# The causal mask of the attention: added by VectorE in the instruction that finds the maximum, instead of by matmuls on TensorE

## The reference

```
for i in range(S // Q_BLOCK):                 # 8 blocks of 128 queries
    q0 = i * Q_BLOCK
    end = q0 + Q_BLOCK                        # keys up to the block's own end
    s = einsum('bqhcd,bkhcd->bhcqk', q[:, q0:end], k[:, :end]) * scale
    causal = kpos[None, :] <= qpos[:, None]
    p = softmax(where(causal, s, -inf), axis=-1)
    w = p[:, :, 0] - lam * p[:, :, 1]
    outs.append(einsum('bhqk,bkhe->bqhe', w, v[:, :end]))
```

## Time and profile before

| | |
|---|---|
| runs | 3737.33, 3740.36, 3741.08 us; median 3740.36 |
| span of the profiled execution, first to last instruction | 3738.0 us |
| the profiled execution's own time | not listed apart from its span; the runs above lie from 0.7 below to 3.1 above that span |
| TensorE busy | 3485.4 us, 93% of the span, 16158 matmuls |
| weight loads | 2816.6 us, beside the matmuls |
| VectorE, ScalarE, GpSimd busy | 1433.6, 829.6 and 949.5 us |
| mean granted TensorE clock | 0.953 of full speed |
| chain of waits, by engine | TensorE 81%, VectorE 12%, ScalarE 2%, issue 2%, DMA 1% |

### The profile page before, as it was taken

How to read it: one execution, slowest core, us unless ns; L and a number is a source line. 1 busy time by engine, 2 the same in 40 slices (tenths; PEclk the granted TensorE clock), 3 DMA queues, 4 the chain that set the end, 5 groups by cost and what they waited for, 6 DMA issues and landing times.

```text
span 3738.0 us, 42270 instructions
## 1 busy us (share of the span) xinstructions
PE 3485.4 (93%) x16158; PEld 2816.6 (75%) x16158; DVE 1433.6 (38%) x1753; ACT 829.6 (22%) x1308; POOL 949.5 (25%) x514
## 2 busy tenths in 40 slices
PE   6888999999889798899999999979999989999999
PEld 5666777777668386677888888868878768888887
DVE  6774444444520557642012222321621543223231
ACT  3332232333320232232122222221110011101010
POOL 2222111111023131112322212224323323333332
PEclk9898999999889799989999999989999989999999
DMA  3432000000001211111121212232111211111112
GB/s 137 126 115 87 23 29 23 23 29 23 12 28 50 107 45 51 51 57 40 50 91 54 66 48 71 52 113 63 50 39 50 86 33 51 45 50 46 49 50 73
DMA packets 83681, 213.93 MB, mean 57 GB/s; under 512 B 7024, under 2 KB 33264, under 8 KB 83456
## 3 DMA queue, kind: packets, MB, share of 16 engines
q1 hardware_dynamic: 48176, 167.27, 14.2%
q10 hardware_dynamic: 35408, 45.24, 3.9%
HBM read 193.44 MB, written 19.04 MB: 57 GB/s over the span
## 4 chain that ended last, share of the span: by engine, by line
PE 81%; DVE 12%; ACT 2%; issue 2%; DMA 1%; PEld 0%; ACTq 0%; DVEq 0%; PEldq 0%; POOL 0%; SPq 0%; POOLq 0%
PE proj_bank L207 20%; PE proj_bank L209 19%; PE proj_bank L208 19%; PE aux_banks L719 3%; PE aux_banks L207 2%; PE aux_banks L209 2%; PE aux_banks L208 2%; PE aux_banks L785 1%; PE aux_banks L729 1%; PE aux_banks L1702 1%; PE aux_banks L514 1%; DVE lru_conv L602 1%; PE aux_banks L1385 1%; PE aux_banks L722 1%; DVE ada_acc L591 1%
## 5 line engine op out<-in xcount | busy, mean ns | idle before, releaser
L207 PE MATMUL proj_bank<-h_hi,slab_hi 128*128 128x512 f32 x2816 | 1131.5, 402 | 36.3 <-DVE h_lo L372 9.1
L208 PE MATMUL proj_bank<-h_lo,slab_hi 128*128 128x512 f32 x2816 | 1111.0, 395 | 0.0
L209 PE MATMUL proj_bank<-h_hi,slab_lo 128*128 128x512 f32 x2816 | 1110.8, 394 | 0.0
L225 POOL CAST slab_hi<-slab_raw 128x1024 fp32r<-128x1024 f32 x255 | 274.3, 1076 | 2745.9 <-PE proj_bank L209 2343.9
L227 POOL TENSOR_TENSOR slab_lo<-slab_raw,slab_hi 128x1024 fp32r<-128x1024 f32 x255 | 675.1, 2647 | 20.4
L207 PEld LDWEIGHTS proj_bank<-h_hi,slab_hi 128*128 128x128 f32 x2816 | 538.6, 191 | 160.1 <-issue 20.2
L209 PEld LDWEIGHTS proj_bank<-h_hi,slab_lo 128*128 128x128 f32 x2816 | 537.6, 191 | 116.3
L208 PEld LDWEIGHTS proj_bank<-h_lo,slab_hi 128*128 128x128 f32 x2816 | 538.7, 191 | 109.8 <-issue 2.2
L207 PE MATMUL proj_bank<-ffn_hi,slab_hi 128*128 128x512 f32 x512 | 199.2, 389 | 0.0
L208 PE MATMUL proj_bank<-ffn_lo,slab_hi 128*128 128x512 f32 x512 | 199.2, 389 | 0.0
L209 PE MATMUL proj_bank<-ffn_hi,slab_lo 128*128 128x512 f32 x512 | 199.2, 389 | 0.0
(11 more groups left out here) (329 smaller groups left out, 4243.3 us busy)
## 6 DMA issues: line engine op xcount, KB each, us to landing
slab_raw<-wts SPq DMA_DIRECT2D x255, 512.0 KB, 3.5
ada_w<-ada_w SPq DMA_DIRECT2D x64, 384.0 KB, 3.1
ssd_decay_rows<-decay_sums ACTq DMA_DIRECT2D x16, 512.0 KB, 4.1
dil_rows<-dilated_out ACTq DMA_DIRECT2D x12, 520.0 KB, 8.0
x_first<-xT SPq DMA_DIRECT2D x4, 1024.0 KB, 9.5
x_again<-xT ACTq DMA_DIRECT2D x4, 1024.0 KB, 10.5
x_kept<-x ACTq DMA_DIRECT2D x8, 512.0 KB, 3.8
mix_kept<-ssd_mix ACTq DMA_DIRECT2D x8, 512.0 KB, 6.4
```

The lines of the kernel that those rows point to most:

```text
L207: pe.matmul(bank, k.whi[:, slot, wk, :], hi[:, xk, cols], start=first and a == 0, stop=False)
L208: pe.matmul(bank, k.whi[:, slot, wk, :], lo[:, xk, cols], start=False, stop=False)
L209: mm = pe.matmul(bank, k.wlo[:, slot, wk, :], hi[:, xk, cols], start=False, stop=last and a == len(ks) - 1)
L225: pool.tensor_copy(k.whi[:, slot], k.raw[:, slot]).then_inc(k.s_hi, 1)
```

## The change

`k.mask` becomes a row of 5 x 128 columns in bf16: four tiles of zeros, and the causal matrix in the last. The mask matmuls are gone. In `maxima` an instruction `tensor_tensor_reduce` adds this row to the last (up to) 640 scores of a component, writes the sums back over the scores in PSUM, and gives their maximum. The zeros stand under the tiles before the own one. Where a step has six tiles or more, a plain reduction of both components' earlier keys comes first, and its result is the starting value of the two fused instructions.

```
-                pe.matmul(own, q, kt[rows, par, i * P:keys], start=True, stop=False)
-                mm = pe.matmul(own, k.mask[:, 0], k.mask[:, 1], start=False, stop=True)
+                mm = pe.matmul(own, q, kt[rows, par, i * P:keys], start=True, stop=True)
                 mm.then_inc(s_score, 1)
...
         def maxima(step, i):
             keys = (i + 1) * P
+            early = max(0, keys - MASK_W)
             flat = score.rearrange("p (c a) b -> p c (a b)", c=2)
+            if early:
+                dve.wait_ge(s_score, step * 2 + 2)
+                v.settle(dve, dve.tensor_reduce(mx[:, 0:2], flat[:, :, 0:early], AX, ALU.max))
+                dve.sem_inc(s_seen, 1)
             for c in range(2):
-                dve.wait_ge(s_score, step * 2 + (c + 1))
-                ins = dve.tensor_reduce(mx[:, c:c + 1], flat[:, c, 0:keys], AX, ALU.max)
+                if not early:
+                    dve.wait_ge(s_score, step * 2 + (c + 1))
+                    dve.sem_inc(s_seen, 1)
+                own = flat[:, c, early:keys]
+                ins = dve.tensor_tensor_reduce(own, own, k.mask[:, MASK_W - (keys - early):], 1.0, mx[:, c:c + 1] if early else LOWEST,
+                                               ALU.add, ALU.max, mx[:, 2 + c:3 + c])
             v.settle(dve, ins)
-            dve.tensor_scalar(nmax, mx, -SCALE, None, ALU.mult).then_inc(s_nmax, 1)
+            dve.tensor_scalar(nmax, mx[:, 2:4], -SCALE, None, ALU.mult).then_inc(s_nmax, 1)
```

The row is made once, at the start of the program, by a memset and a copy, where the two tiles were copied before:

```
-        dve.tensor_copy(k.mask.rearrange("p a b -> p (a b)"), k.const[:, IDENT:CAUSAL + P])
+        dve.memset(k.mask[:, 0:MASK_W - P], 0.0)
+        dve.tensor_copy(k.mask[:, MASK_W - P:], k.causal)
```

More of the change, by code:

```diff
@@ L28 @@
 NEG = -1e30
+LOWEST = -3e38
+MASK_W = 5 * 128
 ADA = 6 * D
@@ L121, in at @@
     def at(name, kb, shape, dt=F32):
-        size = 4 * int(np.prod(shape[1:]))
+        size = (2 if dt == BF16 else 4) * int(np.prod(shape[1:]))
         assert kb * 1024 + size <= k.top, (name, kb, size)
@@ L145, in make_core @@
     k.causal = k.const[:, CAUSAL:CAUSAL + P]
-    k.mask = at("mask_operands", 28.25, [P, 2, P], BF16)
+    k.mask = at("mask_row", 28.75, [P, MASK_W], BF16)
     k.tri = k.const[:, TRI:TRI + P]
@@ L649, in attention_stage @@
     nmax, total, inv, lr = (k.small[:, 48 + 4 * i:50 + 4 * i] for i in range(4))
-    mx = k.small[:, 64:66]
+    mx = k.small[:, 64:68]
     score, turn, out = k.aux[:, 0:4, :], k.aux[:, 4, :], k.aux[:, 5, :]
     s_evac = k.sem("att_evacuated")
-    s_score = k.sem("att_scored")
+    s_score, s_seen = k.sem("att_scored"), k.sem("att_scores_seen")
     s_nmax = k.sem("att_max")
@@ L966, in _ @@
         with dve.Fori(0, (HEADS - 2) // 2) as m:
-            v.enter(m, 2 * TT * 4)
+            v.enter(m, 2 * (TT * 4 + 3))
             for b in range(2):
```

## The result

| | before | after |
|---|---|---|
| time, median (lowest to highest) | 3738.85 us (3737.22 to 3741.08) | 3700.47 us (3696.72 to 3701.61) |
| ratio, 95% interval | | 0.9894 (0.9881 to 0.9907) |
| profiled span | 3738.0 us | 3694.7 us |
| granted clock, mean | 0.953 | 0.954 |

The changed kernel is 1.1% faster. I had forecast 10 us slower; it is 38 us faster.

What follows compares the result with a forecast made beforehand. Heads 0 to 6 were taken as TensorE-bound, with VectorE on head 7's path. The sum was -17.9 (masks) + 19.6 (VectorE) + 3.2 (head 7) + 5 (clock) = +9.9 us, so 3740.4 became 3750 us; range 3730 to 3784.

Steps and rivals of the forecast that it cites:

- the chain's 0.16 each, 0.32 a step: TensorE, two mask matmuls fewer per attention step: 0.16 us each, 17.9 us gained in heads 0 to 6.
- 0.40 a step: TensorE, upper bound per step if the 0.10 us operand change before each mask goes too: 22.4 us in heads 0 to 6.
- the 5 for the clock: TensorE's new waits bring the lower clock level: two episodes of 2.5 us allowed, 5 us lost.
- "faster" rival: Whole kernel: a step saves 0.40 us and the fused instruction runs at the plain reduction's rate, 3731 us; chance 0.17.
- VectorE's cost: Attention steps, fused instructions replacing two reductions: 19.6 us lost in heads 0 to 6, 5.8 in head 7.
- half rate: VectorE, rival: the fused instruction runs at the scan's rate, 1.55 us, giving 3784 us; chance 0.08.
- accumulator read: VectorE, the instruction behind each fused one that reads its accumulator: 0.10 us, between nothing and 0.17.
- low sum of 12.1: Heads 0 to 6, VectorE's loss with low ends (0.82, 0.09, no increment, no collision): 12.1 us.
- new waits: TensorE waiting on VectorE with six, seven and eight key tiles: 0.36 + 0.71 + 1.23 = 2.30 us a head.
- the collision: Seven key tiles: VectorE's two passes over `att_p`, moved later, run into GpSimd's cast; 0.5 us a head.
- The small steps: Steps with one to five key tiles: maximum 0.21 us later, hidden by projection matmuls except in head 7.
- Head 7: Last head, no projection to cover the softmax: 5.8 us lost on VectorE, 2.6 gained from masks, net 3.2 lost.

Runs made afterwards that it cites:

- e5: Kernel before with the mask matmuls left out and nothing in their place, old VectorE reductions kept: 3674.45 us, ratio 0.9827.
- e1: Kernel before with both mask matmuls kept but issued behind the own tiles of both components: 3685.93 us, ratio 0.9868.
- e2: Changed kernel with one mask matmul put back behind component 0, between the two components: 3765.32 us, ratio 1.0083.
- e4: Changed kernel with a mask matmul put back behind each component, so VectorE's part of the change alone: 3770.59 us, ratio 1.0088.

## Why the prediction was wrong, step by step

**The step that failed** is "I take the chain's 0.16 each, 0.32 a step". I priced the removed matmul by its own time on the path. Measured, a step of heads 0 to 6 gains 0.57 (one tile) to 1.42 us (five tiles) and 0.69 to 1.11 (six to eight): 7.7 us a head, 62 in eight heads. e5 puts the whole at 65 us against the 20.5 I had. Its upper bound, 0.40 a step, failed for the same reason: every bound came from rows in which a mask stood between the components, and no such row can show what they do without it. The sum's other terms, with -65 in this one's place, give -65 + 25 = -40 (-35 with the 5 for the clock), and -38 was measured.

The evidence was in the trace, had I asked what two groups of one row had in common. The earlier trace rows have `64*128` for the scores and `128*128` for the mask: two instructions on 64 rows could use the array together, and component 1 starts only at 644.77, behind the mask. My own list of what would prove me wrong named it, "if the first scores of component 1 start before the own tile of component 0 has drained (a larger gain)". I named the observation and gave it neither a price nor a chance. Its price stood in the earlier trace rows: component 1's scores take 1.06 us there (644.77 to 645.83), and laid wholly beside component 0's they would vanish from a step with four key tiles. Measured, that step gained 1.21, mask time included. My "faster" rival, 3731, gave TensorE only the 0.10 us operand change on top. And the assumption that going from 64 rows to other 64 rows is again such a change, by which I chose 0.32, is the opposite of what the runs show.

A page of the Trainium skill states the rule: "TensorEngine Tiling (Array Packing)", section "Key Properties", says that different tiles can load weights and multiply in parallel, and that a change of tiling mode, unlike a change of tile, drains the engine. On the first the traces here agree, with the four matmuls of e1 in 1.14 us. On the second they agree as far as e2's single 128-row matmul sets the components apart again; a drain has no row of its own. Its section "Theoretical Speedup" gives up to 2x for a small dimension of 64 or less, here the contraction. The step with five tiles went from 2.78 to 1.36 us, 2.04 times, the mask's own time included.

**VectorE's cost held in the sum, in part by luck.** I had 19.6 in heads 0 to 6 and 5.8 in head 7, 25 in all. The medians give 26 us (e5 to the changed kernel) and 34 (the kernel before to e4), the profiled attention steps 24.1 and 24.6. By e4, whose TensorE work is that of my sum, it is 16.6 in heads 0 to 6 and 8.0 in head 7: the first came out smaller, the second larger. In its parts:
- The fused instruction: 0.88 forecast, 0.85 to 0.89 measured; half rate is excluded. The accumulator read was put at 0.10; the row has 0.14 (groups by form of the changed kernel), but the next fused instruction starts with it, so only the last one of a step is on the path. (The low sum of 12.1 used 0.09 for this read, though its own low end was nothing.)

```profile
L899 DVE CUSTOM_DVE_ANT_0 aux_banks<-aux_banks,mask_row,small 128x640 f32<-128x640 f32 x48 | 40.7, 890 | 4.5 <-DVE small L892 4.5
L899 DVE DVE_READ_ACCUMULATOR2_ANT small<- 128x1 f32 x128 | 18.1, 142 | 0.0
```

- From the reduction (L892) to the first fused instruction pass 0.19 us, where I had 0.04 + 0.05 for dependence and increment.
- The new waits: 2.30 us a head forecast, 2.80 with the collision: 0.36 with six tiles, 1.21 with seven, 1.23 with eight. In head 2 of the changed kernel TensorE is idle for 2.69 us: 0.36 (for the copy of the turned weights, one tile), 0.56 (on the output's last pass, four tiles), 0.96 (seven) and 0.81 (eight), and nothing with six. The first two aren't VectorE's new work: e5 has 0.36 and 0.43 in the same places without it, because TensorE comes back sooner, while e4 has only the 0.17 of the kernel before with four tiles. The term as I meant it is e4's 1.10 with seven tiles and 0.96 with eight, 2.06 where I had 2.80. That the idle time of heads 1 to 6 rose by 15.6 us where I had 17 is therefore luck in part: e5's rose by 3.8 (4.47 to 8.3), e4's by 13. The wait on the copy of turned values with eight tiles is this one (it answers to the earlier trace rows):

```profile
587.85 0.66 PE L731 MATMUL aux_banks<-const,att_p 128*128 128x128 f32 x4 [0.81 <-DVE att_v L917]
```

- The small steps. With the masks still between the components (e4, head 2) the maximum comes 0.15 to 0.22 us later in the steps with one to five tiles, and 1.40, 1.55 and 1.68 later with six, seven and eight. I had 0.21, and 1.52, 1.64 and 1.78. In the changed kernel both components end together, and component 0's instruction no longer runs beside component 1's scores: there the maximum comes 0.5 to 1.0 us after its old distance from the scores' end (1.5 with four tiles). That is the price of the overlap, and most of it is hidden.
- The collision: 0.5 forecast, 0.65 measured. The pass over `att_p` with seven tiles takes 1.80 us where it took 1.15 (and 1.80 in e4), beside the cast and GpSimd's pass behind it (timelines of VectorE and GpSimd of the changed kernel):

```profile
573.67 1.80 DVE L910 SCALAR_TENSOR_TENSOR att_p<-att_p,small 128x896 f32<-128x896 f32 x1
```

```profile
573.41 1.12 POOL L227 CAST slab_hi<-slab_raw 128x1024 fp32r<-128x1024 f32 x1 [17.38 <-PE proj_bank L211]
574.61 3.07 POOL L229 TENSOR_TENSOR slab_lo<-slab_raw,slab_hi 128x1024 fp32r<-128x1024 f32 x1
```

**Head 7**: 3.2 us slower forecast, 0.4 faster measured. Its waits grew by 6.1 us (5.8 forecast), but TensorE's work fell by 6.5, not 2.6. By e4, VectorE's part alone costs 8.0 there, and by e5 TensorE's part alone gives 4.7.

**The clock**: 5 us lost forecast, nothing lost. Granted clock in heads 1 to 6 was 0.97 before and 0.99 after, with waits of 0.4 to 1 us in each head, so waits of this size didn't bring the lower level here more often. Read in stretches of 5 us, the lower level took some 13 us of full speed from these heads before and 7 after (one minus the granted clock, times the length). About 6 of their 49 us less of busy time are therefore the clock's; the scores' part is 6 x 7.7 = 46, and the small rest goes the other way. Each figure is that of one execution, and over the whole span the mean is the same (0.953 and 0.954), so no clock gain of the change is shown.

## What to carry to other kernels

An instruction removed from a busy engine is worth its own duration plus what it kept apart: look at the tile shapes of the neighbours (64 rows beside 128), and give the case that they now run together a price and a chance. If a change pays by letting two things meet, try first whether the order alone does: moving the two masks behind both components gave 51 us without touching VectorE, where the change of work gave 38. Price the two halves of a change apart too: its sum can come near by errors that cancel. And issue matmuls of the two halves in turn, since three of one half, issued ahead of the other's first, kept it waiting here.

## What the runs showed of the hardware that I hadn't expected

- Two fp32 matmuls on 64 rows each, in different halves of the array, run at the same time to within a few nanoseconds: in the step at 545.36 their starts are 13 ns apart (545.359 and 545.372), and four take 1.14 us where two took 1.12.
- One 128-row matmul of 0.23 us (bf16) between them costs about 1.0 us a step (e2: 65 us for 64 steps).
- The overlap depends on the order of issue. With three matmuls of one half ahead (six in the trace; six key tiles) the other's first begins 0.97 us late (554.72 to 555.69), yet ahead of the third of them (555.90), and the scores take 2.54 us; issued in turn they take 1.57.
- The fused add-and-maximum form, with its output and its input in the same PSUM bank, runs at the plain reduction's rate: 640 elements in 849 to 890 ns, where the reduction took 825. From 256 to 640 columns it adds 1.04 ns a column (448 to 849 ns, groups by form), as the reduction does from 256 to 1024 (424 to 1224).
